# Two maps of differential attention, combined by TensorE while they are turned, instead of by VectorE

## The reference, cut to what matters

```python
def diff_attention(q, k, v, lam, slopes):
    def block(i):
        q0 = i * Q_BLOCK                                    # 128 queries
        qb = lax.dynamic_slice_in_dim(q, q0, Q_BLOCK, axis=1)
        s = jnp.einsum('bqmhd,bkmhd->bmhqk', qb, k, preferred_element_type=jnp.float32) * scale
        s = s - slopes[:, None, None] * dist.astype(jnp.float32)
        s = jnp.where(dist >= 0, s, -jnp.inf)
        p = jax.nn.softmax(s, axis=-1)
        a = p[:, 0] - lam * p[:, 1]
        return jnp.einsum('bhqk,bkhd->bqhd', a.astype(v.dtype), v)
    ...
```

## Time and profile before

| | |
|---|---|
| median of 3 runs | 2295.69 us (2292.41 to 2299.55) |
| profiled execution | 2294.88 us, span 2293.0 us |
| TensorE, VectorE, ScalarE, GpSimd busy over the span | 96%, 55%, 39%, 34% |
| layer 0's attention, 226 to 349 us | TensorE 95.9 us, VectorE 91.2, ScalarE 105.7, GpSimd 46.6 busy of 123 |

### The profile page before, as it was taken

One profiled execution on the slowest core, in us unless ns is written; L12 is line 12 of the kernel. 1 busy time (PEld: TensorE's weight loads), 2 busy tenths in 40 slices (PEclk: granted clock), 3 DMA queues, 4 the chain that ended last, 5 costly groups with the idle time before them and its releaser, 6 DMA issues.

```text
span 2293.0 us, 30307 instructions
## 1 busy us (share of the span) xinstructions
PE 2197.1 (96%) x10416; PEld 1821.6 (79%) x10416; DVE 1271.6 (55%) x1784; ACT 890.4 (39%) x1451; POOL 776.9 (34%) x534
## 2 busy tenths in 40 slices
PE   7999778999999999999999998899999999999999
PEld 6876666888888887888888877787888888887887
DVE  4244776676555555458313236566776555554555
ACT  4123883343333333445311126662443333334433
POOL 0022331167666773002000023220266677662000
PEclk9999999999999999999999998999999999999999
DMA  5021112035555556675111111112035555547665
GB/s 178 10 78 37 38 37 72 3 112 195 192 198 169 170 165 239 194 241 170 37 35 57 37 64 38 24 33 74 19 127 193 194 196 164 167 162 273 192 195 193
DMA packets 217968, 284.83 MB, mean 124 GB/s; under 512 B 11536, under 2 KB 118544, under 8 KB 217872
## 3 DMA queue, kind: packets, MB, share of 16 engines
q1 hardware_dynamic: 217584, 283.55, 38.4%
q10 hardware_dynamic: 288, 0.05, 0.0%
HBM read 199.67 MB, written 73.40 MB: 119 GB/s over the span
## 4 chain that ended last, share of the span: by engine, by line
PE 69%; issue 21%; ACT 4%; DVE 3%; POOL 2%; DMA 0%; POOLq 0%; DVEq 0%; ACTq 0%; SPq 0%
PE PS L1145 12%; PE PS L1144 12%; PE PS L1143 12%; PE PS L1170 6%; PE PS L1172 6%; PE PS L1171 6%; PE PS L904 3%; PE PS L818 3%; PE PS L820 3%; PE PS L819 3%; POOL QRS L771 1%; ACT PR L1364 1%; PE PS L888 1%; PE PS L836 1%; ACT PT L1201 1%
## 5 line engine op out<-in xcount | busy, mean ns | idle before, releaser
L1612 DVE TENSOR_TENSOR LINEl<-LINE,HIGH 128x1024 fp32r<-128x1024 f32 x154 | 194.1, 1266 | 169.3 <-ACT HIGH L1201 169.1
L1201 ACT ACTIVATE HIGH<-LINE 128x1024 fp32r<-128x1024 f32 x154 | 162.5, 1059 | 236.0 <-PE PS L1172 234.0
L1170 PE MATMUL PS<-HIGH 128*128 128x512 f32 x616 | 241.5, 392 | 7.0 <-DVE LINEl L1612 7.0
L1171 PE MATMUL PS<-LINEl,HIGH 128*128 128x512 f32 x616 | 240.6, 391 | 0.0
L1172 PE MATMUL PS<-HIGH,LINEl 128*128 128x512 f32 x616 | 240.6, 391 | 0.0
L1612 DVE TENSOR_TENSOR SLOTl<-BLOCKS,RING 128x512 fp32r<-128x512 f32 x168 | 155.1, 923 | 99.8 <-ACT RING L1201 95.4
L746 POOL TENSOR_TENSOR ST<-ST 128x512 f32<-128x512 f32 x132 | 193.1, 1463 | 32.8 <-DMA ST<-in_ffn_w_down 24.2
L1201 ACT ACTIVATE RING<-BLOCKS 128x512 fp32r<-128x512 f32 x168 | 105.8, 630 | 232.2 <-PE PS L1145 222.0
L771 POOL TENSOR_TENSOR QRS<-QMS,EXPO 128x8 f32<-128x8 f32 x32 | 52.0, 1638 | 383.3 <-DVE QMS L1772 383.2
L1612 DVE TENSOR_TENSOR SLOTl<-SLOT,RING 128x512 fp32r<-128x512 f32 x126 | 132.5, 1051 | 87.5 <-ACT RING L1201 87.3
L904 PE MATMUL PS<-V,PT 128*128 x864 | 117.4, 282 | 26.4 <-ACT PT L1201 23.8
(11 more groups left out here) (278 smaller groups left out, 5615.6 us busy)
## 6 DMA issues: line engine op xcount, KB each, us to landing
LINE<-hidden SPq DMA_DIRECT2D x154, 256.0 KB, 2.7
hidden<-HID SPq DMA_DIRECT2D x44, 512.0 KB, 4.5
ST<-in_ffn_w_down SPq DMA_DIRECT2D x44, 512.0 KB, 4.2
sums<-ST SPq DMA_DIRECT2D x22, 1024.0 KB, 6.2
hidden<-ST SPq DMA_DIRECT2D x22, 1024.0 KB, 6.7
LINE<-sums SPq DMA_DIRECT2D x88, 256.0 KB, 3.0
BLOCKS<-in_ffn_w_gate SPq DMA_DIRECT2D x42, 512.0 KB, 4.0
BLOCKS<-in_ffn_w_up SPq DMA_DIRECT2D x42, 512.0 KB, 5.2
```

The costliest lines, as they stand in the source:

```text
L1170: pe.matmul(dst, hi[:, 0, ts], hi[:, 1, :], start=j == 0 and not adds_on, stop=False, skip_group_check=adds_on)
L1171: pe.matmul(dst, hi[:, 0, ts], lo[:, 1, :], start=False, stop=False, skip_group_check=adds_on)
L1201: return nc.scalar.activation(dst, src, ACT.Copy, **kw)
L1612: return v.tensor_tensor(dst, src, hi.bitcast(F32), ALU.subtract)
```

## The change

For layer 0 `turn` no longer transposes a combined row. For each block it makes two f32 products into the same place in PSUM, the first with `PR[0]`'s block as weights and the identity moving, the second with `PR[1]`'s block as weights and a diagonal matrix `DG` moving, added to the first. `DG` = `IDL` x `RDN` of map 1 x `DEN` of map 0, with `IDL` = -lambda times the identity, made once ahead of the loop. VectorE makes `DG` [128 x 128] in place of `SCB` and of the pass over the row. `PR[1]` is now read by TensorE, so biasing of map 1 waits for the turn as well. `IDL` and the two `DG` lie over the mixer's weights `PW`. Layer 1 is as it was.

```diff
--- before.py
+++ after.py
@@ -224,6 +224,9 @@
         PR = [[at(f"PR{m}{b}", [P, TOK], F32, oHL + 16 * KB + 8 * KB * m + 4 * KB * b) for b in range(2)] for m in range(2)]
         YJ = at("YJ", [P, P], F32, oHL + 12 * KB)
 
+        IDL = at("IDL", [P, P], F32, oK + 4 * KB)
+        DG = [at(f"DG{b}", [P, P], F32, oK + 4 * KB + 512 * (b + 1)) for b in range(2)]
+
         SM = small("SM", 16 + 64)
         SSQ = small("SSQ", NT)
         MSQ = small("MSQ", NT)
@@ -238,7 +241,6 @@
         NMX = small("NMX", 4)
         DEN = small("DEN", 4)
         RDN = small("RDN", 4)
-        SCB = small("SCB", 2)
         YSS = small("YSS", 32)
         YRS = small("YRS", 32)
         LM = small("LM", 6)
@@ -885,8 +887,13 @@
                         else:
                             pe.wait_ge(t_ed[m0][1], h + i0 - 3)
                     for j in range(4 * c, min(4 * c + 4, i + 1)):
-                        last = pe.transpose(turn_bank(L, m, i, c)[:, P * (j - 4 * c):P * (j - 4 * c) + P],
-                                            PR[m][i % 2][:, P * j:P * j + P], IDN[:])
+                        dst, ks = turn_bank(L, m, i, c)[:, P * (j - 4 * c):P * (j - 4 * c) + P], slice(P * j, P * j + P)
+                        if L == 0:
+
+                            pe.matmul(dst, PR[0][i % 2][:, ks], IDN[:], start=True, stop=False)
+                            last = pe.matmul(dst, PR[1][i % 2][:, ks], DG[i % 2][:], start=False, stop=True)
+                        else:
+                            last = pe.transpose(dst, PR[m][i % 2][:, ks], IDN[:])
                 last.then_inc(t_pe[m][L], 1)
 
             def weigh(L, m, u, g, h, i):
@@ -1823,14 +1830,15 @@
                     for c in (1, 3):
                         dve.wait_ge(mx_pe, c + 1)
                         v.tensor_scalar(U[:, c, :], bank(2 * c, 2), PSC[:, c:c + 1], None, ALU.mult).then_inc(mix_ok, 1)
-                per_iter = 2 * (1 + 8 * 2) if L == 0 else 2 * (2 + 16)
+                    dve.wait_ge(idn_ok, 4)
+                    att.did(v.tensor_scalar(IDL[:], IDN[:], LM[:, 5:6], None, ALU.mult))
+                per_iter = 2 * (1 + 8) if L == 0 else 2 * (2 + 16)
                 before = att.n
 
                 def biased(m, b, g, i):
 
                     dve.wait_ge(s_pe[m][L], g + i + 1)
-                    if m <= L:
-                        dve.wait_ge(t_pe[m][L], g + i + 1)
+                    dve.wait_ge(t_pe[m if L else 0][L], g + i + 1)
                     dve.sem_inc(waited[0], 1)
                     b, t = (b, i) if i < NT else (1 - b, i - NT)
                     keys, c = P * (t + 1), m + 2 * (t % 2)
@@ -1861,11 +1869,8 @@
                             dve.wait_ge(s_ex[1][0], g + i + 1)
                             dve.wait_ge(o_ok[0][0], g + i + 1)
                             att.link(v.reciprocal(RDN[:, c0:c0 + 2], DEN[:, c0:c0 + 2]))
-                            att.link(v.tensor_scalar(SCB[:, i % 2:i % 2 + 1], RDN[:, c0 + 1:c0 + 2], DEN[:, c0:c0 + 1], LM[:, 5:6],
-                                                     ALU.mult, ALU.mult))
-                            ks = slice(0, P * (i + 1))
-                            v.scalar_tensor_tensor(out=PR[0][i % 2][:, ks], in0=PR[1][i % 2][:, ks], scalar=SCB[:, i % 2:i % 2 + 1],
-                                                   in1=PR[0][i % 2][:, ks], op0=ALU.mult, op1=ALU.add).then_inc(c_ok, 1)
+                            v.tensor_scalar(DG[i % 2][:], IDL[:], RDN[:, c0 + 1:c0 + 2], DEN[:, c0:c0 + 1], ALU.mult,
+                                            ALU.mult).then_inc(c_ok, 1)
 
                         def scaled(m, i):
```

## The result

The changed kernel takes 2321.0 us in the median (2316.1 to 2327.3, four runs) against 2295.8 for the one before: 1.011 times as long, 95% interval 1.0093 to 1.0127, or 25 us more. On a second occasion it was 2321.3 against 2295.4, with the same interval.

The account below looks back on a forecast made before the run. The prediction took TensorE's copy-to-turn loop in layer 0's attention to bound the changed kernel's later rows: 2294.9 + 26.3 uncovered products + 0.9 clock = 2322.1, forecast 2322.5 us, own range 2316 to 2330, wider 2311 to 2333.

Parts of the forecast that it names:

- The bound: Layer 0's attention, 123 us: no engine full, ScalarE nearest; TensorE waits for VectorE's combining only 1.9 us in all.
- The price of a product: TensorE's turning: an f32 product is two records, 0.223 us, against 0.110 for a transpose; at most 48.2 us over four units.
- The cover, row by row: Copy-to-copy time beyond TensorE's own loop hides added products; what shows is 6.6 us per unit, 26.3 for four.
- The worth of VectorE's relief: VectorE without SCB and combining: some 28 us less busy, but no gain from turn 3 on, where TensorE comes later.
- ScalarE's row before turn 6: Covering row of copy, stack copies, exponentials and scaling: about 4.9 us against TensorE's loop of 5.6, which stays later narrowly.
- The 28 us that VectorE was to save: Busy time VectorE loses in layer 0's attention with SCB and the combining gone and DG added.
- The diagonal: VectorE's making of DG, 128 columns: 0.35 us taken, between SCB's 0.272 and the 128-column combining's 0.756.
- The clock: First unit's turn 1 at 1.2 GHz: 0.9 us added with longer row 0; last unit's last turn: 0 taken.
- Cheap products: Rival 1: products with the identity are one record each, 0.110 us; 2298 to 2299 us, no change; chance 5%.
- More stretches of lower clock in the stage: Rival 2: lower clock in the last rows of more units, 15 us more in three units; 2337 us; chance 6%.
- A better overlap: Rival 3: shorter VectorE row hides half of turns 3 to 5; 2316 us, could reach 2311; chance 10%.
- Four transposes for a product: Rival 4: a product costs four transposes, 0.44 us; 12.8 us per unit more, 2373 us or above; chance 1%.

Follow-up runs that it names:

- x2: Changed kernel plus a third f32 product with an all-zero matrix for each block; 2351.8 us.
- x8: Changed kernel with exponentials, identity and diagonal in reduced-precision fp32r, so each product is one record; 2300.0 us, 1.0022 times the kernel before.
- x6: Kernel before with the change in rows 0 to 2 only; 2296.1 us against 2295.2, ratio 1.0004.
- x7: Kernel before with the change in row 7 only; 2310.8 us.
- x12: x3 with GpSimd's subtractions for the next unit cut to 16 columns (all in second and fourth unit, queries only in first and third); 2339.6 us.
- x3: Changed kernel with VectorE still making SCB and the pass over the row, into scratch, ahead of the diagonal; 2359.7 us.
- x5: Kernel before, VectorE combining as there, with layer 0's row turned by one f32 product with the identity per block instead of a transpose; 2305.9 us.
- x4: Changed kernel with VectorE still making SCB and the pass, but behind the diagonal; 2324.6 us.
- x9: x3 with the identity times -lambda stored with every second element left out, so the diagonal's read is strided, and bfloat16 scratch; 2355.8 us.

## Why the prediction was right, and where it wasn't

- The bound. Read by stage and waits, not by the whole run's 96%: right. The wait for the combining was 1.9 us in all before, and taking it away made no turn at full clock shorter than in the second unit of the kernel before.
- The price of a product. 0.223 us from counting the weighing's records: x2 measures 0.223 us per block; x8 halves the records and gets most of the cost back, 21 of 25 us.
- The cover, row by row. Turns 3 to 7 were summed late by 0.22, 1.35, 1.13, 1.09 and 2.69 us. Measured, third unit: 0.19, 1.43, 1.28, 1.13 and 2.72. Sum with the early turns 6.6 against 6.65, and 6.76 against the second unit. x6 (rows 0 to 2 free) and x7 (row 7 bare, 2.69) bear out both ends of it.
- The worth of VectorE's relief. Here a sentence was wrong though the sum came out: "from turn 3 on ... the gain there is nothing". Against the kernel before it is nothing. But the 6.6 us hold only because VectorE was relieved at the same time. x12, where it isn't and GpSimd is nearly out of the way, has units of 41.3; x3, with GpSimd, 48.5. (Both carry the pass and the diagonal, 0.34 us per row more than the kernel before.) The cover was taken as ScalarE's alone, and x5 shows that VectorE's row was almost as late. In the changed kernel the pass is gone from that row, so the mistake cost nothing there, which is luck: VectorE's row was never summed. In x5 it cost 1.1 us per unit at full clock. In x3 it cost 3.5 of the 10.7 us per unit; the other 7.2 came with the meetings with GpSimd, which the prediction didn't have.
- Slips in the working. 2322.1 + 0.8 is 2322.9 and not 2322.5. ScalarE's row before turn 6 was given as 4.9 us: its terms make 4.7, and the copies stand 4.51 apart there, so the loop of 5.6 was the later one by 1.1, not narrowly. The 28 us that VectorE was to save are the pass alone; with SCB gone and the diagonal added it is 24.5 by groups, and 25.5 in the stage's rows (91.2 to 65.7).
- The diagonal. 0.35 us taken between 0.27 and 0.76; 372 ns in the mean, 346 undisturbed. The high end was misread: 0.756 was the mean of combinings at 128 columns of which the first took 0.35 and the others 0.82 to 0.93, each begun while GpSimd was subtracting, as in the fourth unit of the kernel before:

```profile
318.41 1.80 POOL L781 TENSOR_TENSOR QST<-QK,QST 64x768 fp32r<-64x768 f32 x1 [0.24 <-POOL QST L781]
...
319.44 0.93 DVE L1867 SCALAR_TENSOR_TENSOR PR<-PR,SCB,PR 128x128 f32<-128x128 f32 x1
```

- The clock. The first unit's turn 1 was to run at 1.2 GHz and cost 0.9 with the longer row 0; it ran at full clock (two weights in 0.30 us for two full slots, granted clock of the stretch 0.95 instead of 0.89), and the first full copy is 6.5 us late (262.80 against 256.29), like the others, not 7.5. In the last unit the lower clock of before is gone: the unit is 37.78 where it was 32.58 instead of 31.1, 5.2 us more and not 6.6, so 1.4 us were won back where I took 0 between -0.8 and 3; the -0.8 counted the turn and left out the weighing before it. Both together are the 2 us by which the stage's 25.1 stay under the 27.2 summed.
- The rivals. Cheap products: 0.223, not 0.110. More stretches of lower clock in the stage: fewer. A better overlap: no, turns 4 and 5 came 0.1 later than summed. Four transposes for a product: two, by x2; the section of the Trainium skill named in the prediction gives the ratio of a mode, and at this size a transpose isn't that much faster.

## What to carry to other kernels

Price an operation that moves to another engine by records of the same kind there, and read its cover in each row as the distance between when its successor starts and when it could start, for every engine that stands in front of that successor, not only for the last. Where the receiving engine is near its bound in the long rows, free rows don't pay for them: here 6 of 36 blocks were free and the last 8 cost full price. An engine that is relieved can still matter, by no longer coming late and by no longer meeting another at a shared resource; to see that, put the work back while everything else stays changed.

## What the runs showed of the hardware that I had not expected

A [128 x 128] scaling on VectorE of 0.34 us took up to 2.38 us when it began while GpSimd's two-input subtraction was running, and ended with it (x3; 6.8 us for eight with two long subtractions, 2.4 for seven without, x12). A two-input VectorE pass of 0.75 us took 2.92 when both began within 0.01 us, and when it began 0.12 us ahead it kept its 0.75 and the subtraction took 2.87 instead of 2.36 (x4): with a lead of 0.12 us or more the first wasn't held up. It happens in the kernel before as well, in row 0 (0.35 to 0.93 us for the same pass), and in the changed kernel, whose four longest diagonals took 0.50 to 0.60. The biasing, which reads one operand from PSUM, wasn't held up: 0.68 us, its usual time, at 272.82 us beside a subtraction that began at 272.81.

```profile
272.81 2.37 POOL L784 TENSOR_TENSOR K<-QK,K 64x1024 fp32r<-64x1024 f32 x1 [3.84 <-ACT K L1209]
272.82 0.68 DVE L1847 CUSTOM_DVE_ANT_0 PR<-PS,BIAS 128x512 f32<-128x512 f32 x1
```

By the Trainium skill's lock (SBUF — State Buffer, SBUF: two separate sides) the two-input pass and a two-port scaling wait and the biasing doesn't, and these rows agree. That the scaling waited as long when it read every second element (x9) is a row beside it; whether it was still in a two-port mode no run here shows. Executions of x4 spread over 14 us, those of the other kernels over 4 to 11. That a meeting which hangs on 0.01 us is decided anew in each would explain it; with one trace of x4 it isn't shown.
